# A hybrid decoder step on one core: 1056 instead of 1074 columns in the second half, and the last input chunk contracted row by row

## What is computed

```python
def _mixer(h, st, lead, lb, p):
    z = h @ p['w_in']                                # D 1024 -> 3608 mixer columns + 4096 gate columns
    zh, zr, zg, zm, zgate = _split(z, IN_SIZES)
    ...                                              # HGRN2, RWKV-7, GLA and mLSTM, 256 channels each
    outs = jnp.stack([o_hg, o_rw, o_gl, o_ml], axis=2)
    proj = jnp.einsum('btnc,ncd->btnd', outs, p['w_branch'])
    gates = jax.nn.sigmoid(zgate).reshape(B, T, N_BRANCH, D_MODEL)
    mix = jnp.sum(proj * gates, axis=2) @ p['w_out']
    return mix, new_states

x = x + mix
x = x + jnp.square(jax.nn.relu(rms(x) @ p['w_up'])) @ p['w_down']     # 1024 -> 4096 -> 1024
y_prompt = rms(hp[:, N_META:], norm_final)           # the meta tokens' rows are not returned
```

## Time and profile before

| | |
|---|---|
| time, median of 3 runs | 2366.82 us (2362.13 to 2371.49) |
| time of the profiled execution | 2361.55 us |
| its span, first to last instruction | 2359.8 us |
| mean granted PE clock | 0.962 of full speed |
| busy: PE, PEld, DVE, ACT, POOL | 93%, 89%, 45%, 26%, 20% |
| DMA moved | 178.39 MB |

### The profile page before, as it was taken

How to read it: one execution, slowest core, us unless ns; L and a number is a source line. 1 busy time by engine, 2 the same in 40 slices (tenths; PEclk the granted TensorE clock), 3 DMA queues, 4 the chain that set the end, 5 groups by cost and what they waited for, 6 DMA issues and landing times.

```text
span 2359.8 us, 33482 instructions
## 1 busy us (share of the span) xinstructions
PE 2191.0 (93%) x13459; PEld 2089.3 (89%) x13459; DVE 1055.0 (45%) x1568; ACT 609.2 (26%) x801; POOL 470.5 (20%) x463
## 2 busy tenths in 40 slices
PE   5998998899999888999998789999999999999995
PEld 3987887799999776999998789999999999999994
DVE  4052331566655545333332178642222235655654
ACT  3332221522322143222121143010000013333352
POOL 1121113345553321010000257120000001000012
PEclk9999998999999898999999789999999999999997
DMA  4121113321222231001101365231111224111112
GB/s 153 40 67 57 60 55 99 133 64 60 68 74 83 82 133 42 32 28 37 34 21 37 121 223 191 76 119 45 44 44 42 80 80 192 45 45 44 44 44 83
DMA packets 48563, 178.39 MB, mean 76 GB/s; under 512 B 6401, under 2 KB 6753, under 8 KB 48241
## 3 DMA queue, kind: packets, MB, share of 16 engines
q1 hardware_dynamic: 23040, 85.72, 11.8%
q0 software_dynamic: 17648, 62.03, 7.6%
q10 hardware_dynamic: 7808, 29.71, 3.2%
HBM read 129.41 MB, written 48.02 MB: 75 GB/s over the span
## 4 chain that ended last, share of the span: by engine, by line
PE 85%; DVE 4%; ACT 4%; DMA 3%; issue 2%; POOL 1%; DVEq 0%; SPq 0%; ACTq 0%; POOLq 0%
PE PS L447 26%; PE PS L602 20%; PE PS L1376 15%; PE PS L1338 3%; PE PS L1081 2%; PE PS L1260 2%; PE PS L1256 2%; PE PS L1248 2%; PE PS L1093 1%; DMA RING<-in_w_all 1%; PE PS L948 1%; PE PS L1214 1%; PE PS L1116 1%; PE PS L1222 1%; PE PS L1109 1%
## 5 line engine op out<-in xcount | busy, mean ns | idle before, releaser
L447 PE MATMUL PS<-HT_parts,WHIA_parts 128*128 128x358 f32 x1440 | 513.4, 357 | 35.2 <-POOL RING_parts L442 18.1
L447 PE MATMUL PS<-OT_parts,WHIA_parts 128*128 128x358 f32 x1440 | 480.1, 333 | 0.0
L447 PE MATMUL PS<-HT_parts,RING_parts 128*128 128x358 f32 x1440 | 478.1, 332 | 0.0
L442 POOL TENSOR_TENSOR RING_parts<-RING,WHIA_parts 128x1024 fp32r<-128x1024 f32 x60 | 164.5, 2741 | 838.9 <-ACT WHIA_parts L437 838.9
L447 PEld LDWEIGHTS PS<-HT_parts,WHIA_parts 128*128 128x128 f32 x1440 | 280.0, 194 | 49.7 <-POOL RING_parts L442 19.5
L447 PEld LDWEIGHTS PS<-OT_parts,WHIA_parts 128*128 128x128 f32 x1440 | 279.7, 194 | 3.8 <-issue 0.3
L447 PEld LDWEIGHTS PS<-HT_parts,RING_parts 128*128 128x128 f32 x1440 | 279.1, 194 | 0.0
L1376 PE MATMUL PS<-MIXHI_parts,CF_parts 128*128 128x358 f32 x768 | 251.8, 328 | 3.4 <-DVEq L2507 2.9
L602 PE MATMUL PS<-HT_parts,CF_parts 128*128 128x358 f32 x768 | 251.7, 328 | 0.9 <-ACT AR L569 0.9
L602 PE MATMUL PS<-OT_parts,CF_parts 128*128 128x358 f32 x768 | 251.2, 327 | 0.0
L602 PE MATMUL PS<-HT_parts,RING_parts 128*128 128x358 f32 x768 | 250.8, 327 | 0.0
(11 more groups left out here) (395 smaller groups left out, 3641.2 us busy)
## 6 DMA issues: line engine op xcount, KB each, us to landing
RING<-in_w_all SPq DMA_DIRECT2D x132, 512.0 KB, 3.3
AR<-gates POOLq DMA_DIRECT2D x32, 537.0 KB, 4.0
proj<-AR ACTq DMA_DIRECT2D x18, 537.0 KB, 5.1
AR<-proj POOLq DMA_DIRECT2D x18, 537.0 KB, 8.0
gates<-CF ACTq DMA_DIRECT2D x16, 537.0 KB, 5.1
gates<-AR ACTq DMA_DIRECT2D x16, 537.0 KB, 5.2
AR<-in_xT SPq DMA_DIRECT2D x8, 537.0 KB, 14.1
AR<-in_xT POOLq DMA_DIRECT2D x8, 537.0 KB, 6.9
```

Source lines behind the costliest of these rows:

```text
L442: e.tensor_tensor(RING_R[:, u], RING[:, u], WHIA_R[:, u].bitcast(F32), ALU.subtract).then_inc(S(f"split{u}"), 1)
L447: last = e.matmul(out, a_[:, u, k, :], b_[:, k, t], start=first and i == 0, stop=end and i == 2)
```

## The change

Everything that belongs to the second half leaves out the 16 meta columns and the two of padding: columns 16 to 1071, three groups of G2 = 352. That holds for the gate chunks (pairs 11 to 26, also in the first half), their staging rows, stores and loads, the branches, both projections, the MLP, the norms and y. The mixers' input chunks keep 358.

The last input chunk (pair 26, u = 1) is taken out of the fill work and run at the end, with k outermost and its three column groups in banks 3 to 5; after each k row it counts up `fill_done`, and ACT may then overwrite that row of `HT_R`. The mixers' rows are loaded into a buffer of their own, `MIXRAW`, in the part of the arena that RWKV's scratch no longer needs, and the barrier is gone; semaphores take its place. In the last RWKV tile DVE masks each operand by segment in one instruction, earlier, and empties the nine blocks with three instructions; output and states are reordered, and the fill steps are spread anew. POOL's order becomes: rows, weights' low half, gate rows, state stores.

```diff
+G2 = (NT - META) // 3
+T2 = slice(META, NT)
+        MIXED_ROWS = (0, 1, 4, 5, 6, 7)
+        MIXRAW = Arena(16 * W).take(k=len(MIXED_ROWS), t=W)
...
# fill_work, fill_out (and likewise pe_split_chunk, branches, the down projection)
+                n, t = (G2, part2(g)) if gates else (GRP, slice(g * GRP, (g + 1) * GRP))
                 for k in range(KD):
-                    last = three(e, PS(6 + c % 2, 0, GRP), u, k, slice(g * GRP, (g + 1) * GRP), k == 0, k == KD - 1)
+                    last = three(e, PS(6 + c % 2, 0, n), u, k, t, k == 0, k == KD - 1)
...
# sync queue
+            def last_pieces_read(u, p):
+                e.wait_ge(S("fill_done"), PIECES + KD * u)
-            load_pairs(A["w_br"], P_BR, P_BR + 1, -2 * P_BR, pieces_read)
+            load_pairs(A["w_br"], P_BR, P_BR + 1, -2 * P_BR, last_pieces_read)
...
# POOL
-                for u in range(2):
+                for u in range(2 if q < Q_END - 1 else 1):
                     weight_lo(e, u, P_FILL + q)
-            e.wait_ge(S("fill_done"), Q_END * 6)
-            for k in (0, 1, 4, 5, 6, 7):
-                e.dma_start(OT[:, k], MIXED[k]).then_inc(S("ot_back"), 16)
+            e.wait_ge(S("rw_go"), 2)
+            for k in MIXED_ROWS[:4]:
+                load_mixed(k)
             e.wait_ge(S("states_final"), 3)
-            rw_states(True)
-            barrier(e, 3)
+            for k in MIXED_ROWS[4:]:
+                load_mixed(k)
+            weight_lo(e, 1, P_FILL + Q_END - 1)
             for u in range(2):
-                e.wait_ge(S(f"fill_sent{u}"), Q_END * 16)
+                e.wait_ge(S(f"fill_sent{u}"), (Q_GATE + 2) * 16)
             for c in range(4):
                 zrow(c, c)
+            rw_states(True)
             e.wait_ge(S("out"), 33 * 16)
...
# PE, last RWKV tile and behind it
                 if last_tile:
+                    steps(gate, 5)
                     e.wait_ge(S("rw_vx"), 1)
...
                         if g == 0:
+                            steps(gate, 4)
                             e.wait_ge(S("rw_dsu"), 1)
...
-                steps(gate, 24 if last_tile else 9)
+                steps(gate, 3 if last_tile else 9)
...
-            steps(gate, 96)
-            barrier(e, 3)
+            steps(gate, 72 - (8 + 3 * 6 + 4 + 5 + 4 + 3))
+            e.wait_ge(S("split1"), P_BR)
+            e.wait_ge(S("rw_go"), 2)
+            for k in range(KD):
+                for g in range(3):
+                    last = three(e, PS(3 + g, 0, G2), 1, k, part2(g), k == 0, k == KD - 1)
+                last.then_inc(S("fill_done"), 1)
...
+                    if first and br == 1:
+                        e.wait_ge(S("fill_free"), PIECES + 3)
...
# ACT
-            steps(outs, 12)
-            barrier(e, 3)
+            steps(outs, 5)
+            def hi_row(k):
+                e.wait_ge(S("fill_done"), PIECES + k + 1)
+                if k == 0:
+                    e.wait_ge(S("ot_back"), len(MIXED_ROWS) * 16)
+                    e.wait_ge(S("rw_go"), 2)
+                e.activation(HT_R[:, k, T2], mixed(k)[:, T2], ACT.Copy).then_inc(S("hi_parts"), 1)
+            for k in range(KD - 1):
+                hi_row(k)
+            e.wait_ge(S("fill_done"), PIECES + KD)
+            e.wait_ge(S("fill_sent1"), (Q_END - 1) * 16)
+            e.activation(row2(STAGE_GR[1]), cols2(3), ACT.Copy).then_inc(S("fill_free"), 1)
+            hi_row(KD - 1)
+            e.wait_ge(S("fill_free"), PIECES + 3)
+            e.dma_start(gate_row(31), STAGE_GR[1][:, T2]).then_inc(S("fill_sent1"), 16)
...
# DVE, last RWKV tile and behind it
+                if last_tile:
+                    e.wait_ge(S("rw_kv"), n + 1)
+                    by_segment(RVX, RV)
+                    e.wait_ge(S("rw_us"), n + 1)
+                    by_segment(RUX, RUS).then_inc(S("rw_vx"), 1)
...
+                    blocks(0)
+                    e.sem_inc(S("rw_dsu"), 1)
+                    squares()
+                    st.did(final(0))
+                    scale_rows(n, w)
+                    st.settle()
+                    blocks(1)
+                    output(n, w).then_inc(S("rw_go"), 1)
+                    final(1).then_inc(S("states_final"), 1)
...
-            barrier(e, 3)
-            for u in range(2):
-                e.wait_ge(S(f"fill_sent{u}"), Q_END * 16)
+            e.wait_ge(S("split1"), P_BR)
             split_chunk(e, 0, P_BR)
-            e.wait_ge(S("ot_back"), 6 * 16)
             for k in range(KD):
                 e.wait_ge(S("hi_parts"), KD + k + 1)
-                split_lo(e, OT_R[:, k], HT_R[:, k], mixed(k)).then_inc(S("ot_ready"), 1)
-                if k == 1:
-                    split_chunk(e, 1, P_BR)
+                split_lo(e, OT_R[:, k, T2], HT_R[:, k, T2], mixed(k)[:, T2]).then_inc(S("ot_ready"), 1)
...
+                    if br == 1 and first:
+                        e.wait_ge(S("fill_sent1"), Q_END * 16)
...
+            split_chunk(e, 1, P_BR)
+            e.wait_ge(S("out"), 33 * 16)
             row_muls(0, 0, True)
```

More of the change, by code:

```diff
@@ L471, in fill_work, with fill_out @@
                 yield
-        def fill_out(e, q, c, stage, dst, last=False):
+        def fill_out(e, q, c, stage, dst, last=False, gates=False):
             u, g = divmod(c, 3)
@@ L479, in fill_out @@
             row = stage[u]
-            e.activation(row[:, g * GRP:(g + 1) * GRP], PS(6 + c % 2, 0, GRP), ACT.Copy).then_inc(S("fill_free"), 1)
+            n, t = (G2, part2(g)) if gates else (GRP, slice(g * GRP, (g + 1) * GRP))
+            e.activation(row[:, t], PS(6 + c % 2, 0, n), ACT.Copy).then_inc(S("fill_free"), 1)
             if c == 0:
@@ L539, in sum_pe @@
             for g in range(3):
-                last = e.matmul(PS(bank + g, 0, GRP), ones, sq[:, 0, g * GRP:(g + 1) * GRP], start=True, stop=True)
+                last = e.matmul(PS(bank + g, 0, G2), ones, sq[:, 0, part2(g)], start=True, stop=True)
             last.then_inc(S("sq_used"), 1)
@@ L616, in build @@
         Q_GL_TILES, Q_GL_TAIL, Q_RW_PRE, Q_RW_TILES, Q_RW_TAIL = 9, 17, 18, 21, 25
+        PIECES = 6 * Q_END - 3
         def rw_ti(l):
@@ L896, in pool_program @@
                     e.wait_ge(S(f"mul{br % 2}"), j * 2 + br // 2 + 2)
+                    if j == 1 and br == 0:
+                        for u in range(2):
+                            e.wait_ge(S(f"fill_sent{u}"), Q_END * 16)
                     zrow(j * 4 + 4 + br, br)
@@ L1152, in _ @@
                 with e.Fori(first, end) as n:
-                    gl_tile(n, P, False, fill_work(e, n + Q_GL_TILES))
-            gl_tile(TILES, LASTW, True, fill_work(e, Q_GL_TAIL))
-            gate = chain(*(fill_work(e, q) for q in range(Q_RW_PRE, Q_RW_TILES)))
+                    gl_tile(n, P, False, fill_work(e, n + Q_GL_TILES, first > 0))
+            gl_tile(TILES, LASTW, True, fill_work(e, Q_GL_TAIL, True))
+            gate = chain(*(fill_work(e, q, True) for q in range(Q_RW_PRE, Q_RW_TILES)))
             steps(gate, 48 + 24)
@@ L1317, in _ @@
             with e.Fori(1, TILES // 2) as i:
-                gate = fill_work(e, i + Q_RW_TILES)
+                gate = fill_work(e, i + Q_RW_TILES, True)
                 rw_tile(i * 2, P, False, gate, RC)
                 rw_tile(i * 2 + 1, P, False, gate, RC2)
-            gate = chain(*(fill_work(e, q) for q in range(Q_RW_TAIL, Q_END)))
+            gate = chain(*(fill_work(e, q, True) for q in range(Q_RW_TAIL, Q_END)))
             rw_tile(TILES, LASTW, True, gate, RC)
-            steps(gate, 96)
-            barrier(e, 3)
+            steps(gate, 72 - (8 + 3 * 6 + 4 + 5 + 4 + 3))
[5 more added lines that the diff above has]
+                last.then_inc(S("fill_done"), 1)
             def branches(j, v, first):
@@ L1491, in ml_tile, with outs_of @@
                 steps(outs, 1)
-            def outs_of(q, stage, row, last=False):
+            def outs_of(q, stage, row, last=False, gates=False):
                 for c in range(6):
-                    fill_out(e, q, c, stage, row(c // 3), last)
+                    fill_out(e, q, c, stage, row(c // 3), last, gates)
                     yield
```

155 lines of the change are left out of this document (77 added, 78 removed).

## The result

| | before | after |
|---|---|---|
| median of 4 runs | 2366.14 us (2362.13 to 2371.49) | 2305.25 us (2299.72 to 2313.41) |
| profiled execution | 2361.55 us, span 2359.8 | 2299.72 us, span 2298.2 |
| mean granted PE clock | 0.962 | 0.972 |

The ratio is 0.9743, with a 95% interval of 0.9719 to 0.9767: 61 us less. The lines of the kernel have moved: L447 is now L463 (input chunks), L602 is L623 (up and output projection), L1338 is L1384 (branches), L1376 is L1422 (down projection), L442 is L458 (POOL's split), L1297 is L1333 (state products).

The account below looks back on a forecast made before the run. The matmul engine PE, busy 93% of the span, was taken as the bound. Gains of 4.5 + 41 + 14.3 + 0.3 = 60 us gave 2301.5 or 2307, forecast 2304 between them; own range 2294 to 2312, wider 2290 to 2324.

Parts of the forecast that it names:

- the columns and the transition: 358 columns becoming 352, 4.5 us before and 14.3 us after the transition, plus 0.3; the reworked transition, 41 us.
- Before the transition: Gate chunks in the mixers' tiles and between: 1780 matmuls on the path at 2.5 ns each, 4.5 us saved.
- Price of a column: PE matmuls at the high clock: six columns fewer save 2.5 ns, up to 2.7, or down to 0.
- The last tile and the chunk: Last RWKV tile and last input chunk: tile done at 1311.9, chunk's 72 matmuls at 1323.6, against 1341.7 before.
- the cover of POOL's split: Ahead of the last chunk: GpSimd's weight split is done by 1310, 2 us before PE would wait for it.
- rival (a): Transition keeps a wait, for GpSimd's split or for DVE's store wait and second weight half: 12 us, 2316; chance 0.20.
- Rows in, branches 0 to 2: Rows land at 1311, branches 0 and 1 end at 1329.4, branch 2 starts at 1331 after DVE's product.
- the allowance of 4 us: Taken off the transition's gain for GpSimd and DVE slowing each other, colliding loads and DVE's store wait, leaving 41 us.
- Rival (c): Branch stage: PE stops at DVE's products and the clock stays at 1.2 GHz, 75 us more, 2382; chance 0.04.
- (b): Columns don't count at the high clock, since weight loads set the pace: takes away 19 us, 2323; chance 0.09.
- (d): Transition change misses the path, a store or load still ending where the barrier did: only 19 us, 2345; chance 0.05.
- the wait for the masks: Last RWKV tile: if DVE's wide products take as long as the 18 small ones, 3.5 us of PE's wait stay.

Follow-up runs that it names:

- experiment 2: Changed kernel with all 1074 columns, three groups of 358 from column 0, so only the new transition: 2334.09 us, ratio 0.9834 to the kernel before.
- experiment 5: Changed kernel with up-projection chunk pairs 6 to 10 computing 256 columns a group and pairs 11 to 15 only 128, the rest left out: 2233.59 us.
- Experiment 4: Changed kernel with POOL issuing all six mixers' row loads only when the last chunk is done, own buffer kept: 2328.8 us, ratio 0.9824 to the kernel before.
- experiments 1: Changed kernel with the old transition put back (barrier, late row loads, narrow masks), only the 1056 columns kept: 2350.41 us, ratio 0.9905 to the kernel before.
- experiment 3: Changed kernel with DVE masking the operands in 18 narrow instructions behind the centred rows again: 2320.13 us, ratio 0.9789 to the kernel before.

## Why the prediction was right

The forecast was 2304 us and 60 us less; measured are 2305.25 and 61. Its two parts, the columns and the transition, each gave about what was priced, but single steps were off in both directions, and that the sum came within 1 us is in part luck. By its steps:

**Before the transition**, 4.5 us. The two profiled executions give 5.27, but one pair cannot carry that: executions differ by several us in stretches that the change does not touch. I take the time from the first 120 matmuls of fill work behind the kernel's opening (it starts at 429.31 before and 428.16 after) to the end of the last tile's sums. It is 853.85, 858.36 and 853.39 us in the three profiles with 358 columns (mean 855.2) and 846.78 to 854.83 in eight with 352 (mean 850.6): 4.6 us. The two ranges overlap and the difference is uncertain by some 4 us, so meeting the forecast to the tenth is luck. Nor is it shown that all 1780 matmuls lie on the path: in the 570 us behind that start DVE holds 49 to 65 us of the chain with 358 columns and 61 to 89 with 352, and the granted clock there is not the same in all runs (0.93 in experiment 2, the longest, 0.94 to 0.95 in the others).

**Price of a column.** Taken were 2.5 ns for six columns, measured are 2.96 ns in the up projection (6.62 us over 2232), above the upper bound of 2.7 as well. The surplus of 0.016 us over columns/2.4 grows with the columns, as experiment 5 shows, and is no constant. In the down projection it is less, 1.5 to 1.9 ns in the four pieces of the chain (the second is 88.99 to 88.19 us over 540). The starts there show the same two distances, 0.16 and 0.17, and the cause was not found. Behind the branches the two errors nearly cancel: 12.54 us measured, 13.3 by the prediction's terms (5184 x 2.5 ns + 0.3).

**The last tile and the chunk.** By the steps PE reaches the chunk 28.7 us behind the sums (1311.9 - 1283.2); it does after 29.8 us, mainly since a state product group takes 4.3 us and not 3.9, and then waits 1.07 us. The step that failed is the cover of POOL's split, "2 us", and one of the prediction's own signs of being wrong came with it: PE waits for that split. ACT's high half came 28.3 us behind the sums, where the steps had it after 23.8 (1307 - 1283.2), because its weights' load was asked for at 1296.33, amid the row loads, and landed late; the prediction had no term for it. Experiment 4 shows that it is the row loads. There they come later, and the same weights land in half the time (the landings in the change, 1290 to 1300, and in experiment 4, 1300 to 1312):

```profile
RING<-in_w_all SPq DMA_DIRECT2D x1, 512.0 KB, 8.8
...
RING<-in_w_all SPq DMA_DIRECT2D x1, 512.0 KB, 4.3
```

In experiment 4 PE goes into the chunk without a wait. So this is rival (a) with a price of 1 us in place of 12.

**Rows in, branches 0 to 2.** The last of the six rows landed at 1307.86, before the chunk began, and branch 0 followed the chunk without a gap. Branch 2 waited for the product behind the second weight half, as forecast, and came 49.59 us behind the sums where the steps said 47.8. The difference of 1.8 us is no more than what the chunk came late, and the allowance of 4 us covers it. That allowance was taken off for collisions that were named and not sized; that some 3 us of it were needed is luck.

**Branch stage.** Forecast were 1.35 us for the columns and 1.7 for the half-clock stretch, measured are 1.85 together. The half-clock stretch is gone, but PE stops a little more than before. Its waits behind the start of branch 2, before (1376 to 1468) and after (1328 to 1419), as total, number and longest, and a group of DVE after:

```profile
PE PS L1338 <- DVE AR L2416: 0.9, 2, 0.4
...
PE PS L1384 <- DVE AR L2476: 1.3, 3, 0.5
...
L597 DVE CAST CF_parts<-RING 128x1024 fp32r<-128x1024 f32 x7 | 11.1, 1593 | 3.6 <-DMA RING<-in_w_br 3.6
```

PE waits 1.3 us for DVE's products, 0.4 us more than before, and the starts around each stop are far apart as well: by the distances of starts all of this takes 3.2 us, before 2.3 beside the half-clock stretch. The products stand behind casts and splits of branch weights that come 4.7 us after they are asked for. Rival (c) foresaw these stops, but the fall that it expected of them did not come: the clock of this stage is 0.97 to 1.00 in every profile here.

**Rivals.** (b) falls at these widths with experiments 1 and 5, (d) with 4, (c) with the clock of the stage. What the prediction priced too low is the wait for the masks: it put 3.5 us on their taking as long as before, and experiment 3 measured 12.6, since 9 us of clock come on top of the wait.

Taken back one at a time, the early loads are worth 18.0 us, the wide masks 12.6, the loop order 3.6, each by one profile (the masks' by two). The ratios of the whole kernels say 19, 11 and 4 us, each to some 8 us. If the parts add up, which was not tried, that leaves 7.7 of the 41.9 us for the rest (barrier and drains, orders of POOL and DVE), which was not split further.

## What to carry to other kernels

Look at what a stall does to the clock behind it before pricing it: a wait of 3 us in front of a dense stretch cost 12.6 here. Where an all-engine barrier stands between two stages that share a buffer, the early loads into a buffer of their own gave the largest part of the gain, 18 of 42 us, and contracting the last reader row by row another 3.6. Loads that are moved forward meet other loads there: the weights that the last chunk needed landed after 8.8 us instead of 4.3. Columns that nobody reads are worth their full share of PE's time as long as the pace is set by columns; a look at the pace at two or three widths says whether it is.

## What was not expected of the hardware

- The matmul pace at full clock is 1.10 to 1.11 times columns/2.4 GHz from 256 to 358 columns (0.119, 0.162, 0.165 us), and 0.112 us at 128; at half clock it was columns/1.2, 0.299 us at 358.
- A wait of 3.27 us was followed by half clock only 1.9 us after PE had started again, for 20.5 us, twice out of twice. Without a wait, the same tile at 358 columns fell once for 17 us and once for 3.4, and with 352 columns it kept 1.00 in all five profiles of the unchanged tile.
- Falls of this kind also come in the mixers' tiles while PE is busy, in other places from run to run. The second experiment's profile has one at 600 and one at 680, as its table by stage shows:

```profile
600.00:610.00 10.00, 10.00 (x62) 9.63 (x61) 6.26 (x21) 3.89 (x5) 3.94 (x2) 0.83 0.03 5
680.00:690.00 10.00, 10.00 (x60) 9.26 (x60) 5.19 (x18) 2.04 (x4) 3.04 (x1) 0.83 0.16 65
```

Its repeat, the same kernel, has neither:

```profile
600.00:610.00 10.00, 9.98 (x69) 9.56 (x68) 8.75 (x27) 5.92 (x8) 5.18 (x2) 1.00 0.10 26
680.00:690.00 10.00, 10.00 (x65) 9.58 (x65) 8.75 (x24) 5.96 (x9) 6.95 (x8) 1.00 0.10 26
```

A clock of 0.83 over 10 us is 3.4 us at half speed, a loss of 1.7. Such falls can be part of why executions of one kernel lie 14 us apart (2299.72 to 2313.41): the mean granted clocks of these two are 0.972 and 0.969, which is at most some 7 us of PE's time. What makes the rest is not known.
